# Where four operand buffers begin in each partition of the on-chip memory

## The reference

```python
def modulated(x, mod, gains, j):
    return rms_norm(x, gains[j]) * (1.0 + mod[:, :, 3 * j + 1]) + mod[:, :, 3 * j]

def swiglu(h, w_in, w_out):
    g, u = jnp.split(h @ w_in, 2, axis=-1)
    return (jax.nn.silu(g) * u) @ w_out

def half_ffn(x, mod, gains, j, w_in, w_out):
    return x + FFN_RES * mod[:, :, 3 * j + 2] * swiglu(modulated(x, mod, gains, j), w_in, w_out)
```

## Time and profile before

| what | value |
|---|---|
| three executions | 1665.81, 1669.05, 1669.52 us (median 1669.05) |
| the profiled execution, first to last instruction (its span) | 1668.0 us |
| PE busy | 1537.1 us, 92% of the span |
| DVE busy | 1192.3 us, 71% |
| ACT busy | 624.6 us, 37% |
| mean granted TensorE clock | 0.955 |

### The profile page before, as it was taken

How to read it: one execution, slowest core, us unless ns; L and a number is a source line. 1 busy time by engine, 2 the same in 40 slices (tenths; PEclk the granted TensorE clock), 3 DMA queues, 4 the chain that set the end, 5 groups by cost and what they waited for, 6 DMA issues and landing times.

```text
span 1668.0 us, 24331 instructions
## 1 busy us (share of the span) xinstructions
PE 1537.1 (92%) x8554; PEld 1500.3 (90%) x8554; DVE 1192.3 (71%) x1745; ACT 624.6 (37%) x876; POOL 329.4 (20%) x377
## 2 busy tenths in 40 slices
PE   6899999999636899999989999998989899999997
PEld 6899999989626899999989999997869889999997
DVE  6877779976799787779978777897766565444432
ACT  1433332244873343332243333224544534333321
POOL 5000003300224300002310000140376440000021
PEclk9999999989768899999989999998989999999998
DMA  8555566624212365566636556663322133333431
GB/s 331 170 199 189 189 214 223 212 94 139 92 46 87 105 203 189 189 211 222 220 115 220 187 189 214 199 217 124 100 76 66 62 96 95 126 126 130 155 104 38
DMA packets 67074, 256.96 MB, mean 154 GB/s; under 512 B 7472, under 2 KB 8496, under 8 KB 66640
## 3 DMA queue, kind: packets, MB, share of 16 engines
q1 hardware_dynamic: 47680, 187.57, 33.5%
q0 software_dynamic: 18432, 67.12, 12.2%
q10 hardware_dynamic: 912, 1.65, 0.3%
HBM read 253.68 MB, written 2.63 MB: 154 GB/s over the span
## 4 chain that ended last, share of the span: by engine, by line
PE 73%; DVE 15%; issue 5%; POOL 3%; ACT 3%; DMA 2%; SPq 0%; DVEq 0%; ACTq 0%; POOLq 0%
PE bank L531 21%; PE bank L533 21%; PE bank L532 20%; DVE wide L1110 4%; DVE wide L1113 3%; PE bank L569 2%; PE bank L570 2%; PE bank L573 2%; DVE w_lo_sb L1091 1%; DVE gv L1410 1%; PE wide L712 1%; DMA ada_raw<-in_ada_w 1%; DMA x<-in_x 1%; ACT w_hi_sb L814 1%; DVE x L1252 1%
## 5 line engine op out<-in xcount | busy, mean ns | idle before, releaser
L1091 DVE TENSOR_TENSOR w_lo_sb<-raw,w_hi_sb 128x1024 fp32r<-128x1024 f32 (+2 forms) x304 | 428.4, 1410 | 172.9 <-ACT w_hi_sb L814 167.5
L531 PE MATMUL bank<-h_hi,w_hi_sb 128*128 128x384 f32 x1620 | 546.3, 337 | 3.0 <-DVEq L1530 3.0
L533 PE MATMUL bank<-h_hi,w_lo_sb 128*128 128x384 f32 x1620 | 544.9, 336 | 0.0
L532 PE MATMUL bank<-h_lo,w_hi_sb 128*128 128x384 f32 x1620 | 544.9, 336 | 0.0
L814 ACT ACTIVATE w_hi_sb<-raw 128x1024 fp32r<-128x1024 f32 (+2 forms) x304 | 343.3, 1133 | 536.7 <-PE bank L533 528.6
L531 PEld LDWEIGHTS bank<-h_hi,w_hi_sb 128*128 128x128 f32 x1620 | 305.1, 188 | 4.9 <-DVEq L1530 3.2
L532 PEld LDWEIGHTS bank<-h_lo,w_hi_sb 128*128 128x128 f32 x1620 | 305.1, 188 | 0.1
L533 PEld LDWEIGHTS bank<-h_hi,w_lo_sb 128*128 128x128 f32 x1620 | 305.0, 188 | 0.0
L531 PE MATMUL bank<-a_hi,w_hi_sb 128*128 128x384 f32 x704 | 237.1, 337 | 3.3 <-DVEq L1271 1.8
L533 PE MATMUL bank<-a_hi,w_lo_sb 128*128 128x384 f32 x704 | 236.6, 336 | 0.0
L532 PE MATMUL bank<-a_lo,w_hi_sb 128*128 128x384 f32 x704 | 236.6, 336 | 0.0
(11 more groups left out here) (239 smaller groups left out, 1650.3 us busy)
## 6 DMA issues: line engine op xcount, KB each, us to landing
raw<-in_ffn_in SPq DMA_DIRECT2D x176, 512.0 KB, 3.4
ada_raw<-in_ada_w POOLq DMA_DIRECT2D x128, 512.0 KB, 3.6
raw<-in_ffn_out SPq DMA_DIRECT2D x64, 704.0 KB, 4.1
raw<-in_rg_in SPq DMA_DIRECT2D x20, 512.0 KB, 3.4
ada_first<-in_ada_w SPq DMA_DIRECT2D x8, 1024.0 KB, 17.4
raw<-in_rg_out SPq DMA_DIRECT2D x8, 640.0 KB, 3.9
raw<-in_gla_qk SPq DMA_DIRECT2D x8, 512.0 KB, 4.0
raw<-in_gla_v SPq DMA_DIRECT2D x8, 512.0 KB, 3.4
```

What stands on the lines that cost most here:

```text
L531: pe.matmul(out, w_hi_sb[:, slot, w], hi[k], start=start and j == 0, stop=False)
L532: pe.matmul(out, w_hi_sb[:, slot, w], lo[k], start=False, stop=False)
L533: last = pe.matmul(out, w_lo_sb[:, slot, w], hi[k], start=False, stop=stop and j == len(ks) - 1)
L1091: V.tensor_tensor(w_lo_sb[:, s, 0:w], raw[:, s, 0:w], w_hi_sb[:, s, 0:w].bitcast(F32), ALU.subtract).then_inc(w_split, 1)
```

## The change

A helper `moving` allocates a buffer that is `skip` elements longer than needed and returns the part behind the first `skip` elements, in the old shape. The four buffers `h_hi`, `h_lo`, `a_hi` and `a_lo` are made with it, with 12 elements (48 bytes) each. `span_all` grows by 64 elements (256 bytes), which moves the five buffers behind it by 256 bytes. No instruction is added, removed or reordered.

```diff
+        def moving(name, chunks, skip, scope):
+
+            whole = sb(name, [P, skip + chunks * T], F32R, scope)
+            return whole[:, skip:skip + chunks * T].rearrange("p (k t) -> p k t", t=T)
+
         hbuf_scope = ExitStack()
-        h_hi = sb("h_hi", [P, DC, T], F32R, hbuf_scope)
-        h_lo = sb("h_lo", [P, DC, T], F32R, hbuf_scope)
+        h_hi = moving("h_hi", DC, 12, hbuf_scope)
+        h_lo = moving("h_lo", DC, 12, hbuf_scope)
         ffn_scope = ExitStack()
-        a_hi = sb("a_hi", [P, FC, T], F32R, ffn_scope)
-        a_lo = sb("a_lo", [P, FC, T], F32R, ffn_scope)
+        a_hi = moving("a_hi", FC, 12, ffn_scope)
+        a_lo = moving("a_lo", FC, 12, ffn_scope)
...
-        sb("span_all", [P, 2 * DC * T + 2 * FC * T], F32, ctx)
+        sb("span_all", [P, 2 * DC * T + 2 * FC * T + 64], F32, ctx)
```

## The result

The changed kernel is slower: 1675.98 us (median of five runs, 1674.26 to 1676.76) against 1668.88 us for the kernel before in the same comparison. The ratio is 1.0047, 95% interval 1.0035 to 1.0059.

A forecast was written before the change was run, and what follows sets the result against it. TensorE's stream of matmuls, busy 92% of the span at 173.3 ns per product, was taken as the bound. 1668.0 - 22.5 = 1645.5 us for the profiled execution, stated as 1647; range 1600 to 1692 and a little over.

The forecast's parts named there:

- Step 1: The four buffers: beginnings move from 96 to 16 and 80 behind a multiple of 128 bytes, no instruction added or removed.
- Step 2: Products of `tile`: 170 ns each instead of 173.3, -3.3 ns, since streams meet less from odd multiples of 16 bytes.
- Step 3: Products that gain: 6972 in `tile` plus 24 with `wz` less 192 of r blocks, 6804; times -3.3 ns, -22.5 us.
- Step 4: FFN: nothing hides the gain in input products; in output products VectorE has 6 of 92 us free, so it fits.
- Step 5: Engines writing the buffers (ACT, VectorE) and DMAs behind `span_all`: no effect, writers within 0.5 us of either sign.
- Unlocked: Rival, `tile` products: jumps between high and low cost 1.7 or 3.4 ns each, 1681 or 1692 us; chance 0.35.
- Locked again: Rival, `tile` products: streams settle at the same distance from any constant beginning, 173.3 ns, 1669 us; chance 0.17.
- all of it goes: Rival, `tile` products: excess vanishes, 160 ns each, -90 us, 1578; only the tail of the forecast's own case.

The follow-up runs named there:

- h_only: Changed kernel with the 48 bytes ahead of `h_hi` and `h_lo` only, `a_hi` and `a_lo` at 96 again: 1682.88 us, one run.
- the maps: Bare streams of 384-column products, no whole kernel, over pairs of high and low buffer places, some with other `w_lo` places or product order: minimum 171.1 ns in each 256-place map.
- the map: Bare stream, 24 products for each of 1024 pairs of high and low places 16 bytes apart, weights fixed: 171.1 to 180.0 ns per product, median 175.5.
- the table of equal places: Bare stream with high and low buffer at one place, 32 places in two orders, 48 products each: 173.3 ns at 224, 180.0 at 240.
- all_at_16: Kernel before with all four buffers 16 behind a multiple of 128, high and low equal: 1678.85 us against 1668.43, ratio 1.0056.
- h_at_240: Kernel before with `h_hi` and `h_lo` moved 16 bytes to 240/240, `a` by 32 to 0/0: 1701.41 us, ratio 1.0194.
- the last bare stream: Products alone, 14 pairs of places, each entered six times after a pause of about 4 us, 96 products each: 192/240 took 1.62 or 1.54 us for nine.
- h_pair_only: Kernel before with `h` at 192/240 and `a` at 0/0: 1668.47 us, ratio 0.9994, twelve runs between 1654.12 and 1679.34.

## Why the prediction was wrong

- **Step 1 held in what it moved, not in the cycle.** The beginnings are 16 and 80 behind a multiple of 128 and no instruction differs. But the cycle is 256 bytes. In it the old place is 224, and the change puts `h` and `a` at different pairs. The step also left out that `xc`, `xc_hi` and `xc_lo` move by 128 bytes, which cost nothing. A trace with one set of places couldn't show the cycle; h_only did, and the maps measured it.
- **Step 2 failed: the price per product.** It took 170 ns, -3.3 ns from 173.3; measured are 175.1 to 175.6 in the map and +2.0 to +2.2 ns in the stretches, so its term of -22.5 us had the wrong sign (the medians moved by +7.1). Two things were wrong in it. The idea that odd multiples of 16 bytes part the two streams is contradicted by the table of equal places: of the even multiples 0, 32, 64, 160 and 224 give 173.3 in both orders and 192 in one (96 and 128 don't), while of the odd ones 16, 48, 144, 176, 208 and 240 give 174.5 to 180.0; only 112 reaches 173.3 in both orders and 80 in one. And the number came from the shortest single distances of the earlier trace rows, although the same rows average 173.8. The averages of the earlier trace rows, 176.7, 173.8 and 175.0, all lay above 173.3. Read as three samples of other places, they said that the old place was cheap; of the 256 pairs three quarters are dearer than 173.5.
- **Step 3 (count) held for `tile`.** The input products carry the price evenly. It was too generous as a multiplier: 6804 x 2.1 ns would be +14 us, the medians show +7.1, because the stretches outside the FFNs and the output products of FFN 0 and 2 gave some back.
- **Step 4 (what hides it) was right in its rows for the input products and incomplete for the output products.** Nothing hides a longer product in the former. In the output products the 6 us of room of VectorE were weighed only against a gain; for a loss they work the other way, and in FFN 0 TensorE's idle time shrank by 1.0 us within the output product.
- **Step 5 (writers) held**: VectorE's busy time is 1193.6 us against 1192.3, ACT's 624.5 against 624.6.
- **The rivals.** That 1675.98 us lies inside the stated range isn't the forecast's merit: the range reaches above 1669 for *Unlocked*'s sake. *Unlocked* had the right sign, and its two prices (1.7 and 3.4 ns) enclose the measured 2.0 to 2.2. Its reason, the jump between high and low, did not hold: all_at_16 has no jump and loses 0.56%. *Locked again* got something right for many other places (173.3 is the commonest low rhythm), not for these. That *all of it goes* has no support: none of some 2900 combinations of places in the maps has a mean below 171.1 ns.

The Trainium skill, TensorE: Matmul & The Clock Gate, "Step-by-step: what each phase is for", says that a weight load takes no read bandwidth from the running product, since the engine has two independent read ports. These runs don't agree with what I drew from it, no effect of an address: 16 bytes cost 6.7 ns on 173.3. They don't show either that the ports are what collides.

**What stays open.** Whether two streams meet, which two, and in what unit, isn't shown; the maps give times by place, no cause. Steps below 16 bytes, other lengths than 384 columns and 16-bit operands weren't tried. Why 192/240 enters one rhythm or the other isn't known, nor why the clock stayed up longer after FFN 0, nor what the moves change outside the FFNs' products. How the weights' own beginning enters was measured at a few places only.

## What to carry to other kernels

Where a kernel is a long stream of matmuls, read the distance of their starts over many products, not their durations and never single distances, and compare it with columns by clock: what is left over can depend on where the operands begin. Map the places with a bare stream that uses the kernel's own shapes and order, keep the weights where the kernel has them, choose a pair that is cheap from many entries, and time the kernel in many runs: a pair with several rhythms shows as spread, and a few entries can miss one. And a buffer added or resized ahead of the operands moves them: 16 bytes on `h` (with 32 on what lies behind, whose FFN products kept their time) cost this kernel 1.9%, with no instruction changed, so a comparison of two versions should hold the places fixed.

## What was unexpected of the hardware

- At the granted clock 1.00 the mean distance of 384-column products lay between 171.1 and 184.4 ns by the beginnings of the operands alone, in a cycle of 256 bytes. In the map of pairs the commonest values are 173.3, 174.4, 175.6, 176.7 and 177.8, each 1.1 ns from the next.
- At 0.50 no place that was tried costs anything: 320 ns in the kernel before, in `h_at_240` with `h` at 240/240 (from 345.32 to 347.24 us, six products), and in every entry of the last bare stream.
- The same instructions in the same places can run for a thousand products at 180.0 ns and, entered again, at 171.1 (`h_pair_only`).
